# Expert weights of a mixture layer: the low halves written over the lower 16 bits of the fp32 words, and twelve raw buffers in place of eight

## What is computed

```python
def moe_swiglu(h, router, w1, w3, w2):
    logits = jnp.einsum('bld,de->ble', h, router, preferred_element_type=F32)
    top_v, top_i = lax.top_k(logits, TOP_K)            # TOP_K = 2
    wts = jax.nn.softmax(top_v, axis=-1)
    gates = jnp.sum(jax.nn.one_hot(top_i, N_EXPERTS, dtype=F32) * wts[..., None], axis=-2)
    y = jnp.zeros_like(h)
    for e in range(N_EXPERTS):                          # 8
        y = y + gates[..., e:e + 1].astype(h.dtype) * swiglu(h, w1[e], w3[e], w2[e])
    return y
# swiglu(h, w1, w3, w2) = (silu(h @ w1) * (h @ w3)) @ w2; w1, w3: 1024 x 2816, w2: 2816 x 1024, all fp32
```

## Time and profile before

| what | value |
|---|---|
| median of 3 runs | 1839.96 us (1839.65 to 1841.42) |
| the profiled execution, first to last instruction (its span) | 1838.2 us |
| what the median has beside the span | 1.8 us |
| TensorE busy | 96% of the span |
| DVE busy | 63% of the span |
| read from HBM | 405.55 MB |

### The profile page before, as it was taken

The page is one execution under the profiler, slowest core; times in us unless marked ns, Lnnn a source line. Parts: engine busy times, 40 slices in busy tenths (PEclk is TensorE's granted clock), DMA queues, the critical chain, the costliest instruction groups (busy, mean ns, idle before and its releaser), DMA issues.

```text
span 1838.2 us, 34033 instructions
## 1 busy us (share of the span) xinstructions
PE 1769.7 (96%) x14950; PEld 1114.3 (61%) x15001; DVE 1151.5 (63%) x1385; ACT 368.6 (20%) x671; POOL 82.9 (5%) x76
## 2 busy tenths in 40 slices
PE   6999999989999999999999978999999999999998
PEld 2434556674544444445465644878696878778695
DVE  1240176896433323214224696999999999999998
ACT  1101155242422222112013432201101010000000
POOL 0033000020000000000330001000000000000000
PEclk9999999999999999999999999999999999999999
DMA  9832200002445454230221017699999999999994
GB/s 371 309 138 69 92 1 29 18 24 98 174 188 206 183 206 160 94 113 3 89 92 69 1 47 281 255 417 409 418 416 415 418 412 419 413 418 410 412 416 194
DMA packets 98842, 408.72 MB, mean 222 GB/s; under 512 B 14008, under 2 KB 20856, under 8 KB 84368
## 3 DMA queue, kind: packets, MB, share of 16 engines
q1 hardware_dynamic: 96504, 405.54, 56.0%
q10 hardware_dynamic: 2200, 1.08, 0.2%
HBM read 405.55 MB, written 1.05 MB: 221 GB/s over the span
## 4 chain that ended last, share of the span: by engine, by line
PE 79%; DVE 10%; DMA 4%; issue 3%; ACT 2%; PEld 1%; ACTq 0%; PEldq 0%; DVEq 0%; SPq 0%; POOL 0%; POOLq 0%
PE PS L1548 12%; PE PS L1924 10%; PE PS L710 9%; PE PS L708 8%; PE PS L1506 6%; PE PS L1898 5%; PE PS L1900 5%; PE PS L1901 5%; DMA ARENA<-in_moe_w 3%; DVE ARENA L2020 2%; PE PS L454 2%; PE PS L1412 2%; PE PS L1274 2%; DVE ARENA L908 2%; DVE ARENA L905 1%
## 5 line engine op out<-in xcount | busy, mean ns | idle before, releaser
L2020 DVE TENSOR_TENSOR ARENA<-ARENA 128x2816 bf16<-128x2816 f32 (+2 forms) x184 | 567.3, 3122 | 23.1 <-DMA ARENA<-in_moe_w 22.6
L1898 PE MATMUL PS<-ARENA 128*128 128x96 bf16 x2816 | 378.6, 209 | 5.8 <-DVE ARENA L2020 3.0
L1900 PE MATMUL PS<-ARENA 128*128 128x96 bf16 x2816 | 378.4, 209 | 1.7 <-issue 1.7
L1901 PE MATMUL PS<-ARENA 128*128 128x96 bf16 x2816 | 378.3, 206 | 0.4 <-issue 0.2
L1900 PEld LDWEIGHTS PS<-ARENA 128*128 128x128 bf16 x2816 | 354.7, 126 | 8.8 <-issue 8.6
L1898 PEld LDWEIGHTS PS<-ARENA 128*128 128x128 bf16 x2816 | 346.3, 123 | 11.8 <-issue 7.5
L1901 PEld LDWEIGHTS PS<-ARENA 128*128 128x128 bf16 x2816 | 298.4, 106 | 2.5 <-issue 2.4
L710 PE MATMUL PS<-ARENA 128*128 128x512 f32 (+1 forms) x608 | 236.9, 530 | 1.3 <-DVE ARENA L623 1.3
L1924 PE MATMUL PS<-ARENA 128*96 128x512 bf16 x960 | 216.1, 384 | 0.4 <-DVE ARENA L2020 0.4
L1548 PE MATMUL PS<-ARENA 128*128 128x512 bf16 x960 | 213.5, 379 | 1.7 <-issue 0.6
L1924 PEld LDWEIGHTS PS<-ARENA 128*96 128x96 bf16 x960 | 116.2, 122 | 93.7 <-issue 0.8
(11 more groups left out here) (242 smaller groups left out, 1704.4 us busy)
## 6 DMA issues: line engine op xcount, KB each, us to landing
ARENA<-in_moe_w SPq DMA_DIRECT2D x128, 1408.0 KB, 13.9
ARENA<-in_moe_w SPq DMA_DIRECT2D x48, 1536.0 KB, 16.0
ARENA<-in_ada_w SPq DMA_DIRECT2D x24, 2048.0 KB, 10.1
ARENA<-in_ffn_w SPq DMA_DIRECT2D x15, 2048.0 KB, 7.8
ARENA<-in_w_in SPq DMA_DIRECT2D x11, 2048.0 KB, 7.9
ARENA<-in_moe_w SPq DMA_DIRECT2D x16, 1024.0 KB, 16.0
ARENA<-in_w_in SPq DMA_DIRECT2D x6, 1024.0 KB, 7.0
ARENA<-in_w_out SPq DMA_DIRECT2D x8, 512.0 KB, 4.5
```

What stands on the lines that cost most here:

```text
L1898: pe.matmul(out, hi[:, h][:, f], HEH[:, k, :], start=k == 0 and b % 4 == 0, stop=False, skip_group_check=True)
L1900: pe.matmul(out, hi[:, h][:, f], HEL[:, k, :], start=False, stop=False, skip_group_check=True)
L1901: mm = pe.matmul(out, lo[:, h][:, f], HEH[:, k, :], start=False, stop=k == KC - 1, skip_group_check=True)
L2020: dve.tensor_tensor(WLO[q % NSLOT][:, 0:n], RAW[q % NSLOT][:, 0:n], WHI[q % NSLOT][:, 0:n], ALU.subtract).then_inc(S("m_lo"), 1)
```

## The change

The low half of a word is written over its own lower 16 bits: WLO becomes the other half of the same view as WHI. So dve_low reads and writes the same buffer, with a step of two bf16 elements in its output, and the eight buffers of WLO are gone. Their space, and other tiles moved closer together, gives twelve raw buffers. SP loads twelve pieces ahead of the loop, and in the loop it waits for the piece twelve back.

```diff
-        NPIECE, NSLOT = 24, 8
+        NPIECE, NSLOT = 24, 12
         HALF, HB = D_FF // 2, FC // 2
-        RAW = [A(at, 3 * D) for at in (40, 52, 64, 76, 96, 108, 0, 12)]
-        EARLY = 6
-        WHI = [v.bitcast(BF16).rearrange("p (n two) -> p n two", two=2)[:, :, 1] for v in RAW]
-        WLO = [A(at, 3 * D // 2).bitcast(BF16) for at in (88, 120, 24, 30, 126, 132, 138, 144)]
+        RAW = [A(at, 3 * D) for at in (48, 60, 72, 96, 108, 84, 0, 12, 120, 132, 24, 36)]
+        WHI, WLO = ([v.bitcast(BF16).rearrange("p (n two) -> p n two", two=2)[:, :, part] for v in RAW] for part in (1, 0))
+        RAW_FULL = [(f"m_raw{s}", 0) for s in range(8)] + [(f"ring_full_{x}", loads[x]) for x in ("E0", "E1", "E2", "H0")]
+        FIRST_FREE = {0: [("o_mixed", since(1, "o_mixed") + 2)], 5: [("o_tp", since(1, "o_tp") + 2)],
+                      6: [("out_mm", since(1, "out_mm") + 4)], 10: [("norm_tp", 4 * KC)]}
...
-        def sp_slot_free(sp, i, q):
-
-            if q < 8:
-                sp.wait_ge(S("m_used"), USED * i + 13 + q)
+        def sp_consumed(sp, i, q):
+
+            if q >= 16:
+                sp.wait_ge(S("m_used"), USED * i + USED + 12 + q - 16 + 1)
             elif q % 4 == 3:
-                sp.wait_ge(S("m_full"), FULL * i + 3 * (q // 4 - 1))
+                sp.wait_ge(S("m_full"), FULL * i + 3 * (q // 4 + 1))
             else:
-                sp.wait_ge(S("m_used"), USED * i + USED + 3 * (q // 4 - 2) + q % 4 + 1)
...
+                sp.wait_ge(S("m_used"), USED * i + USED + 3 * (q // 4) + q % 4 + 1)
...
         def sp_moe(sp):
-            sp.wait_ge(S("o_mixed"), since(1, "o_mixed") + 2)
             for q in range(NSLOT):
-                sp_piece(sp, 0, 0, q, first=True)
+                for sem, value in FIRST_FREE.get(q, ()):
+                    sp.wait_ge(S(sem), value)
+                sp_piece(sp, 0, q)
...
                 for q in range(NSLOT, NPIECE):
-                    sp_piece(sp, i, e, q)
+                    sp_consumed(sp, i, q - NSLOT)
+                    sp_piece(sp, e, q)
                 for q in range(NSLOT):
-                    sp_piece(sp, i + 1, later, q)
+                    sp_consumed(sp, i, q + NSLOT)
+                    sp_piece(sp, later, q)
```

More of the change, by code:

```diff
@@ L1627, in trunk @@
         SLOTS = 96
-        NPIECE, NSLOT = 24, 8
+        NPIECE, NSLOT = 24, 12
         HALF, HB = D_FF // 2, FC // 2
-        RAW = [A(at, 3 * D) for at in (40, 52, 64, 76, 96, 108, 0, 12)]
-        EARLY = 6
-        WHI = [v.bitcast(BF16).rearrange("p (n two) -> p n two", two=2)[:, :, 1] for v in RAW]
-        WLO = [A(at, 3 * D // 2).bitcast(BF16) for at in (88, 120, 24, 30, 126, 132, 138, 144)]
-        UA = [A(150, HB * SLOTS), A(154.125, HB * SLOTS)]
+        RAW = [A(at, 3 * D) for at in (48, 60, 72, 96, 108, 84, 0, 12, 120, 132, 24, 36)]
[3 more added lines that the diff above has]
+                      6: [("out_mm", since(1, "out_mm") + 4)], 10: [("norm_tp", 4 * KC)]}
+        UA = [A(144, HB * SLOTS), A(148.125, HB * SLOTS)]
         AEH = [v.bitcast(BF16).rearrange("p (n two) -> p n two", two=2)[:, :, 1] for v in UA]
-        AEL = [A(158.25, HB * SLOTS // 2).bitcast(BF16), A(36, HB * SLOTS // 2).bitcast(BF16)]
-        HEH, HEL = [A(at, KC * SLOTS // 2).bitcast(BF16).rearrange("p (k s) -> p k s", k=KC) for at in (38.0625, 94)]
-        PG = [A(39.5625, SLOTS), A(95.5, SLOTS)]
+        AEL = [A(at, HB * SLOTS // 2).bitcast(BF16) for at in (152.25, 154.3125)]
+        HEH, HEL = [A(at, KC * SLOTS // 2).bitcast(BF16).rearrange("p (k s) -> p k s", k=KC) for at in (156.375, 157.875)]
+        PG = [A(159.375, SLOTS), A(159.75, SLOTS)]
         MOLD = BYTES
@@ L1815, in split_pieces, with raw_landed @@
             return sum(p not in DIRECT for p in range(q))
+        def raw_landed(eng, i, q):
+            sem, before = RAW_FULL[q % NSLOT]
+            eng.wait_ge(S(sem), before + 16 * (NPIECE // NSLOT * i + q // NSLOT + 1))
         def low_ready(pe, i, q):
             if q in DIRECT:
-                pe.wait_ge(S(f"m_raw{q % NSLOT}"), 16 * (3 * i + q // NSLOT + 1))
+                raw_landed(pe, i, q)
             else:
@@ L1826, in piece_words, with sp_piece @@
             return 2 * HALF if q < 16 else D * (YBLOCKS[q - 16][1] - YBLOCKS[q - 16][0])
-        def sp_slot_free(sp, i, q):
-            if q < 8:
-                sp.wait_ge(S("m_used"), USED * i + 13 + q)
+        def sp_consumed(sp, i, q):
+            if q >= 16:
+                sp.wait_ge(S("m_used"), USED * i + USED + 12 + q - 16 + 1)
             elif q % 4 == 3:
-                sp.wait_ge(S("m_full"), FULL * i + 3 * (q // 4 - 1))
+                sp.wait_ge(S("m_full"), FULL * i + 3 * (q // 4 + 1))
             else:
-                sp.wait_ge(S("m_used"), USED * i + USED + 3 * (q // 4 - 2) + q % 4 + 1)
[L1837 to L1842, removed]
+                sp.wait_ge(S("m_used"), USED * i + USED + 3 * (q // 4) + q % 4 + 1)
+        def sp_piece(sp, e, q):
             if q == 16:
@@ L1855, in sp_piece @@
                 dst = RAW[q % NSLOT][:, 0:D * (c1 - c0)].rearrange("p (c n) -> p c n", n=D)
-            sp.dma_start(dst, src).then_inc(S(f"m_raw{q % NSLOT}"), 16)
+            sp.dma_start(dst, src).then_inc(S(RAW_FULL[q % NSLOT][0]), 16)
         def sp_moe(sp):
-            sp.wait_ge(S("o_mixed"), since(1, "o_mixed") + 2)
             for q in range(NSLOT):
-                sp_piece(sp, 0, 0, q, first=True)
+                for sem, value in FIRST_FREE.get(q, ()):
+                    sp.wait_ge(S(sem), value)
+                sp_piece(sp, 0, q)
             sp.wait_ge(S("r_rounds"), 1)
@@ L1866, in sp_moe @@
                 for q in range(NSLOT, NPIECE):
-                    sp_piece(sp, i, e, q)
+                    sp_consumed(sp, i, q - NSLOT)
+                    sp_piece(sp, e, q)
                 for q in range(NSLOT):
-                    sp_piece(sp, i + 1, later, q)
+                    sp_consumed(sp, i, q + NSLOT)
+                    sp_piece(sp, later, q)
             for q in range(NSLOT, NPIECE):
-                sp_piece(sp, last, N_EXP - 1, q)
+                sp_consumed(sp, last, q - NSLOT)
+                sp_piece(sp, N_EXP - 1, q)
         def pe_gather(pe, i):
@@ L2018, in dve_low @@
             n = piece_words(q)
-            dve.wait_ge(S(f"m_raw{q % NSLOT}"), 16 * (3 * i + q // NSLOT + 1))
+            raw_landed(dve, i, q)
             dve.tensor_tensor(WLO[q % NSLOT][:, 0:n], RAW[q % NSLOT][:, 0:n], WHI[q % NSLOT][:, 0:n],
```

## The result

| | before | changed |
|---|---|---|
| median | 1840.69 us (1839.65 to 1842.61, 4 runs) | 1896.95 us (1896.41 to 1897.97, 4 runs) |
| span of the profiled execution | 1838.2 us | 1895.1 us |
| ratio to before | | 1.0305, 95% interval 1.0291 to 1.0319 |

The change makes the kernel 3% slower, where 0.37% was forecast (1847 us, range 1841 to 1853). The prediction was wrong. The first view to read is again that of the experts, here the first four, from TensorE's first matmul of each; the columns are those of the earlier trace rows.

The account below looks back on a forecast made before the run. The prediction took TensorE's own pace to bound the kernel. Its terms, -4.2 (waits gone) + 7.9 (weight loads) + 3.2 (moving operand) = +6.9 us, gave 1847 us, 0.37% slower, range 1841 to 1853.

Parts of the forecast that it names:

- What costs nothing: DVE's low halves, SP's DMAs and instruction fetches: stepped output leaves DVE's instruction as long as before; 0 us taken.
- The cover: DVE's idle time in an expert: 23 low halves may each grow 0.18 us (6%) before DVE sets the pace.
- signs of being wrong: Profile signs: L1901's load stays at 106 ns, L2020 grows over 6%, or an expert's time follows the landings.
- DVE slows on stepped output: Rival: DVE's low halves grow over 6%; at 14%, 46 us more, near 1893 us; chance 0.03.
- The gain of twelve slots: Expert stage: last landing 14.2 us earlier, but only TensorE's waits for DVE go, 4.2 us gained.
- The loads of the low weights: L1901 in blocks 0 to 8: step goes from 6 to 12 bytes, 3.45 ns more per load, 7.9 us lost.
- one of the two bounds named: L1901's loads: low load's slack lets high loads catch up; a triple takes 153 ns, 43 us lost.
- The moving operand: L1924 streams the low half with a 4-byte step: 10 ns for each of 320 matmuls, 3.2 us lost.
- the transfers didn't set the end: Rival that the queues are the true bound: the end comes 14.2 us earlier, 1826 us; chance 0.03.
- stepped reads do cost: Rival that TensorE's stepped reads cost nothing more: only 4.2 us gained, 1835.8 us; chance 0.08.
- only the loads cost: Rival that TensorE's low weight loads cost, its streaming nothing: +3.7 us, 1843.7 us; chance 0.12.

Follow-up runs that it names:

- m1: Kernel before, with DVE subtractions of 2816 elements appended behind its end, alone and beside other work: 4-byte-step bf16 output 3.27 us alone, 3.52 to 3.69 beside TensorE, dense 3.09.
- m2: Kernel before, with DVE subtractions into six output forms appended, alone and beside TensorE's 12-byte loads: half-word bf16 outputs 3.27 us alone; pairs and fp32 3.09 in both.
- h2: Changed kernel, one matmul of each triple left out, TensorE reading high halves for low, DVE making half of each low half: 1816.6 us, ratio 0.9872.
- h3: Kernel before (eight slots), one matmul of each triple left out, TensorE reading high halves for low, DVE making half of each low half: 1830.2 us, ratio 0.9943.
- e1: Changed kernel, but low halves written densely over the raw buffer, in consecutive bf16 words, and read so by TensorE: 1839.1 us, ratio 0.999.
- e3: Changed kernel, with DVE making only half of each low half and TensorE multiplying the high half in the low one's place: 1846.2 us, ratio 1.0028.
- e4: Kernel before (eight slots, dense low halves), with TensorE multiplying the high half in the low one's place: 1847.2 us, ratio 1.0034.
- p1: Changed kernel, with four of an expert's low halves (pieces 5, 9, 13, 17) made by GpSimd in place of DVE: 1909.6 us, ratio 1.0376.

## Why the prediction was wrong

**The step that failed** is "What costs nothing", the sentence "I take no growth". It rested on rows in which the output is dense bf16 or whole fp32 words, and carried them over to single 16-bit pieces of words, of which there was no row. In its place the runs showed 3.27 us alone and 3.52 to 3.69 beside TensorE for 2816 elements, where dense takes 3.09 (m1, m2), and 3.62 in the kernel. The cover was computed rightly: 6% before DVE sets the pace. The growth was 17%; more than 6% was one of the signs of being wrong that the prediction named itself.

**The rival that came true** is "DVE slows on stepped output", with a chance of 0.03. Its far bound, the 14% of COPY_PREDICATED, priced it at 1893 us; measured were 17% and 1897. That they lie close is luck: the row of another instruction and another length bounds nothing, and the growth went past it. A form without a row, with a cover of only 6% and 46 us behind it, deserved more than 0.03.

**The gain of twelve slots** had the right mechanism: transfers 14 us earlier (13.6 between h2 and h3), worth only TensorE's few us of waits as long as TensorE is the bound (2.0 by the medians of e1, 4.2 forecast). In the changed kernel itself DVE was the bound, and of the earlier landings nothing was left.

**The loads of the low weights** were mis-sized. Three 12-byte loads in a row take 140 ns and not 138: by the means over the stage 139.9 - 134.5 = 5.4 ns for each of 2304 triples, 12.4 us in place of 7.9. That a third slow load slows the other two a little (the high ones start 46 to 47 ns apart) was one of the two bounds named, far below its 43 us.

**The moving operand** was right: 84 matmuls of L1930 in 18.93 us against 18.67 for the same 84 before, 3.1 ns each, 3.0 us over 960; forecast 3.2.

**Left out of the sum** were TensorE's own short stops, put down to "issue". Measured from start to start among the matmuls of pieces 0 to 15, as far as they exceed the pace of 45 ns, stops over 0.15 us added up to 10.4 us in the expert stage before, 4.2 of them waits for low halves and 6.1 issue; in e3 all together are 1.5. So some 4.6 us of issue stops vanish, which is why 12.4 + 3.0 - 4.2 - 4.6 = 6.6 us ends close to the forecast 6.9 and to e3's span (+6.5). That the forecast for TensorE fits so well is thus luck: one term was too small by 4.5 us, and the one left out is of the same size. The issue stops go with TensorE's pace and not with the slots: 8.2 us in e1 (twelve slots, 134.7 ns a triple), 2.0 in e4 (eight slots, 139.9 ns). What causes them stays open.

**The other rivals:** the transfers didn't set the end (in e1 they land 13.4 us earlier and the time is 2.0 us less); stepped reads do cost (e3, e4); "only the loads cost" is out, as the moving operand costs its 3 us.

**A smaller loss behind DVE's.** Six times in the loop, each time around a wait of TensorE of 1.8 to 2.2 us, its granted clock fell to 0.50, that is 1.2 GHz, for 3.4 us, and its matmuls then start 80 ns apart. Other waits as long brought no fall. One of the six, in the columns of the earlier trace rows:

```profile
1308.60:1310.30 1.70, 1.70 (x25) 1.70 (x23) 1.70 (x1) 0.00 (x0) 0.00 (x0) 0.50 1.02 417
```

DVE stays fully busy through it, so it costs nothing as long as DVE is the bound. The accounting above (57.0 us from DVE beside 56.9 measured) leaves little room for more. One thing no run shows: the time of a kernel that does all the work with DVE relieved and nothing else burdened. The runs that relieve DVE (e3) or undo the step (e1) do not compute the right result.

## What to carry to other kernels

An engine that is busy 96% of the loop, as DVE was, has a cover of 4%; any edit of its instructions' operands, a step in the output too, has to be priced with a row of just that form, and where there is none, measured by itself before the layout is built on it. Write whole 4-byte words from DVE: a bf16 result packed into the free half of an fp32 word saves space and cost 6 to 19% of the instruction here. More buffers bring transfers forward by the stretch that was empty, but the time only by what the bound engine waits.

## What the runs showed of the hardware

- A DVE output of single bf16 elements, one in every second word (8-byte step), takes 6.43 us for 2816, twice the dense 3.09, while fp32 with the same 8-byte step takes 3.09 (m1, m2).
- Of the forms measured, only the half-word outputs are disturbed by TensorE at work, with any step of its reads: 3.27 us goes to 3.52 to 3.69. Transfers from HBM at 362 GB/s beside it do nothing (3.27). The Trainium skill (SBUF — State Buffer, Who interferes with whom) knows of contention only in the port pair that DVE and GpSimd share; for the transfers the trace agrees, for a half-word output beside TensorE it does not, and the measurement decides.
- A weight load with a step of 12 bytes spaces matmuls of 96 columns at 46 to 47 ns, steps of 8 bytes and less at 42.5. The Trainium skill's rule of two hits on a line (Advanced Engine Details and Errata, SBUF Cachelines) agrees with where the loss begins. It does not cover the moving operand, whose 4-byte step costs 10 ns from start to start (225 in place of 215), nor DVE's output, where the same 4-byte step is free for fp32 and not for bf16.
- A GpSimd tensor_tensor of two SBUF operands and DVE's take turns, an instruction at a time (p1). One low half on DVE that meets it takes 7.0 to 8.4 us in place of 3.6, and one on GpSimd takes 4.9 to 22.3 us, with 4.9 of its own. DVE waits for at most one of GpSimd's instructions, GpSimd for up to four of DVE's in a row, until DVE has one that reads PSUM. The section Who interferes with whom of the Trainium skill (SBUF — State Buffer) says that a DVE instruction with two SBUF inputs contends with a GpSimd one that reads SBUF, and the trace agrees with it.
